# The first mixer of a one-core block: decay matrices applied one slot later, by 64 weight columns to their own half of the partitions

## What is computed

```python
def step(state, inp):                                   # chunks of 128 positions
    xc, dtc, lac, bc, cc = inp
    cum = jnp.cumsum(lac, axis=1)
    decay = jnp.exp(jnp.where(causal, cum[:, :, None] - cum[:, None], -jnp.inf))
    xdt = xc * dtc[..., None]
    cb = jnp.einsum('blgn,bsgn->blsg', cc, bc)
    y = jnp.einsum('blsgr,bsgrp->blgrp', cb[..., None] * decay, xdt)
    y = y + jnp.einsum('blgn,bgrpn->blgrp', cc, state) * jnp.exp(cum)[..., None]
    ...
```

## Time and profile before

| | us |
|---|---|
| median of 3 runs | 1860.97 (1857.37 to 1861.91) |
| profiled execution, device time | 1857.3 |
| its span | 1855.6 |
| TensorE matmul busy | 1735.0 (94%) |
| VectorE busy | 1189.9 (64%) |
| ScalarE busy | 769.0 (41%) |
| GpSimd busy | 408.1 (22%) |
| mean granted clock of TensorE | 0.983 |

### The profile page before, as it was taken

How to read it: one execution, slowest core, us unless ns; L and a number is a source line. 1 busy time by engine, 2 the same in 40 slices (tenths; PEclk the granted TensorE clock), 3 DMA queues, 4 the chain that set the end, 5 groups by cost and what they waited for, 6 DMA issues and landing times.

```text
span 1855.6 us, 21247 instructions
## 1 busy us (share of the span) xinstructions
PE 1735.0 (94%) x8104; PEld 1404.2 (76%) x8104; DVE 1189.9 (64%) x1587; ACT 769.0 (41%) x1143; POOL 408.1 (22%) x351
## 2 busy tenths in 40 slices
PE   6989999999987999999999889999999999999997
PEld 4767777787765777878777677888778778888886
DVE  6868878877966747575757676777665553434343
ACT  5333444343343435444445344446454442324232
POOL 0444644653563100000002501222120110000001
PEclk9989999999988999999999899999999999999999
DMA  3312222222210322222212223222323233333331
GB/s 102 91 35 68 67 70 57 60 66 69 57 49 25 86 54 65 80 79 69 76 54 87 63 74 80 62 59 80 103 82 103 88 91 91 103 91 102 92 101 69
DMA packets 253772, 139.18 MB, mean 75 GB/s; under 512 B 26013, under 2 KB 248134, under 8 KB 253670
## 3 DMA queue, kind: packets, MB, share of 16 engines
q1 hardware_dynamic: 253670, 137.82, 26.1%
HBM read 135.70 MB, written 2.10 MB: 74 GB/s over the span
## 4 chain that ended last, share of the span: by engine, by line
PE 58%; DVE 22%; ACT 9%; issue 7%; POOL 4%; DMA 1%; ACTq 0%; DVEq 0%; SPq 0%; POOLq 0%
PE stream L79 16%; PE stream L81 16%; PE stream L80 16%; DVE weights_lo L147 3%; ACT weights_hi L137 2%; DVE ssd_x L983 2%; DVE ssd_work L1061 1%; DVE ssd_bc L983 1%; DVE ssd_work L1057 1%; DVE ssd_y L1088 1%; PE q L1978 1%; PE q L2002 1%; POOL ssd_y L653 1%; PE q L79 1%; PE q L81 1%
## 5 line engine op out<-in xcount | busy, mean ns | idle before, releaser
L79 PE MATMUL stream<-u_lo,weights_hi 128*128 128x512 f32 (+2 forms) x1312 | 525.3, 400 | 17.0 <-DVE h L952 5.1
L81 PE MATMUL stream<-u_hi,weights_hi 128*128 128x512 f32 (+2 forms) x1312 | 514.7, 392 | 0.0
L80 PE MATMUL stream<-u_hi,weights_lo 128*128 128x512 f32 (+2 forms) x1312 | 514.6, 392 | 0.0
L147 DVE TENSOR_TENSOR weights_lo<-weights_raw,weights_hi 128x1024 fp32r<-128x1024 f32 (+4 forms) x269 | 336.3, 1252 | 270.2 <-ACT weights_hi L137 269.9
L137 ACT ACTIVATE weights_hi<-weights_raw 128x1024 fp32r<-128x1024 f32 (+4 forms) x269 | 268.5, 1000 | 444.9 <-PE stream L81 430.4
L79 PEld LDWEIGHTS stream<-u_lo,weights_hi 128*128 128x128 f32 (+2 forms) x1312 | 247.7, 189 | 81.0 <-issue 12.4
L81 PEld LDWEIGHTS stream<-u_hi,weights_hi 128*128 128x128 f32 (+2 forms) x1312 | 247.3, 188 | 54.2 <-issue 0.4
L80 PEld LDWEIGHTS stream<-u_hi,weights_lo 128*128 128x128 f32 (+2 forms) x1312 | 247.4, 189 | 53.9 <-issue 2.9
L217 POOL COPY h_sum_of_squares<-h_squares 128x512 f32<-128x512 f32 x5 | 3.2, 648 | 796.9 <-ACT h_squares L205 796.9
L79 PE MATMUL stream<-mlp_a_lo,weights_hi 128*128 128x512 f32 x256 | 100.2, 391 | 0.0
L81 PE MATMUL stream<-mlp_a_hi,weights_hi 128*128 128x512 f32 x256 | 99.7, 389 | 0.0
(11 more groups left out here) (484 smaller groups left out, 3155.9 us busy)
## 6 DMA issues: line engine op xcount, KB each, us to landing
weights_raw<-in_w_mlp_dram SPq DMA_DIRECT2D x64, 512.0 KB, 4.0
weights_raw<-in_ssd_w_in_dram SPq DMA_DIRECT2D x48, 512.0 KB, 3.9
weights_raw<-in_gla_w_in_dram SPq DMA_DIRECT2D x40, 512.0 KB, 3.8
weights_raw<-in_w_in_dram SPq DMA_DIRECT2D x29, 512.0 KB, 3.8
weights_raw<-in_ssd_w_out_dram SPq DMA_DIRECT2D x16, 512.0 KB, 3.6
weights_raw<-in_gla_w_out_dram SPq DMA_DIRECT2D x13, 512.0 KB, 3.4
weights_raw<-in_w_out_dram SPq DMA_DIRECT2D x8, 512.0 KB, 3.9
weights_raw<-in_w_xkv_dram SPq DMA_DIRECT2D x8, 512.0 KB, 3.8
```

The lines of the kernel that those rows point to most:

```text
L79: pe.matmul(out, lh, rl, start=first, stop=False, skip_group_check=skip)
L80: pe.matmul(out, ll, rh, start=False, stop=False, skip_group_check=skip)
L81: return pe.matmul(out, lh, rh, start=False, stop=last, skip_group_check=skip)
L147: dve.tensor_tensor(lo, raw_view(c, n), hi.bitcast(F32), ALU.subtract).then_inc(c.w_split, 1)
```

## The change

In `y_intra`, `y_intra(g, t)` is called in slot t + 3 instead of t + 2: slots 3 to 6. Each product now has the head's own 64 columns as stationary operand and writes 64 partitions of the bank, 0 to 63 for the first head of a pair and 64 to 127 for the second; none adds to another. `x_pair` loses its zeros (128 columns a pair), the copies into it become two instead of four, the semaphore counts on them follow, and GpSimd's clear and its semaphore go.

```diff
-        xp = mb("x_pair", [P, NT, 2, 192])
+        xp = mb("x_pair", [P, NT, 2, P])
...
-            pool.memset(xp[:, :, :, 64:128], 0.0).then_inc(s_clear, 1)
...
             def y_intra(g, t):
                 pe.wait_ge(s_m, 3 * (4 * g + t + 1))
                 if t == 0:
-                    pe.wait_ge(s_xp, 5 * g + 5)
+                    pe.wait_ge(s_xp, 3 * g + 3)
                     pe.wait_ge(s_xw, 4 * g + 4)
                 for p in range(2):
                     for h in range(2):
-                        a = slice(64 * h, 64 * h + P)
-                        last = pe.matmul(q[p][:, t * P:(t + 1) * P], xp[:, t, p, a], mm[:, t % 2, 2 * p + h, :],
-                                         start=h == 0, stop=h == 1, skip_group_check=True)
+                        a = slice(HD * h, HD * (h + 1))
+                        last = pe.matmul(q[p][a, t * P:(t + 1) * P], xp[:, t, p, a], mm[:, t % 2, 2 * p + h, :],
+                                         start=True, stop=True, skip_group_check=True)
                 last.then_inc(s_y, 1)
...
-                if 2 <= k <= 5:
-                    y_intra(g, k - 2)
+                if 3 <= k <= 6:
+                    y_intra(g, k - 3)
...
-                    act.wait_ge(s_clear, 1)
                     if g:
                         act.wait_ge(s_y, 4 * g)
                     for b in range(2):
-                        for h in range(2):
-                            src = q[b][:, :].rearrange("p (t j h m) -> p t j h m", t=2, j=2, h=2)[:, :, :, h, :]
-                            act.activation(xp[:, 2 * b:2 * b + 2, :, P * h:P * h + 64], src, ACT.Copy)\
-                               .then_inc(s_xp, 1)
+                        src = q[b][:, :].rearrange("p (t j m) -> p t j m", t=2, j=2)
+                        act.activation(xp[:, 2 * b:2 * b + 2, :, :], src, ACT.Copy).then_inc(s_xp, 1)
...
-                    dve.wait_ge(s_xp, 5 * g + 4)
+                    dve.wait_ge(s_xp, 3 * g + 2)
```

More of the change, by code:

```diff
@@ L596, in ssd_stage @@
          s_arg, s_decay, s_t2, s_m, s_y, s_con, s_st, s_int, s_e, s_ee, s_asm, s_sq, s_nrm,
-         s_rs, s_yn, s_yh, s_yl, s_clear) = (sem(n) for n in (
+         s_rs, s_yn, s_yh, s_yl) = (sem(n) for n in (
              "centre_tap", "taps", "conv_done", "gate_done", "transposed", "cb_products",
@@ L601, in ssd_stage @@
              "states", "y_inter", "cum_spread", "exp_cum_ready", "assembled",
-             "squared", "square_sums", "rstd_ready", "normed", "y_rounded", "y_rest", "cleared"))
+             "squared", "square_sums", "rstd_ready", "normed", "y_rounded", "y_rest"))
         G = range(SG)
```

## The result

| | before | after |
|---|---|---|
| median | 1861.44 (1857.37 to 1863.25, 4 runs) | 1848.21 (1846.92 to 1849.49, 4 runs) |
| profiled execution | 1857.3 | 1846.9 |
| one steady round of the first mixer | 65.74 | 64.39 |

The account below looks back on a forecast made before the run. The prediction took VectorE's stretch from 281 to 300 us of the first mixer's round as the bound; first round 5.8, six rounds 7.8 and last 0.5 made 14.1 us off 1860.97: 1846.9, given as 1846.5, range 1839 to 1856.

Parts of the forecast that it names:

- VectorE is the bound, TensorE's stalls are its shadow: Steady round: VectorE's stretch from 281 to 300 us sets the time; TensorE's 22.8 us of block waits are no gain yet.
- 1.3 us a steady round: Slots 2 to 4: earlier GpSimd steps collide less with VectorE, 1.3 us a round, 7.8 us over six rounds.
- just fits: Fourth block in slot 6 costs 0.81 us; two later TensorE waits for VectorE give back 0.4 each.
- First round 5.8, or 4.4 if the idleness lowers the clock again: First round: decay sums start 4.4 us earlier; 1.4 more if the clock stays at 2.4 GHz, making 5.8.
- Last round 0.5: Last round: L724 no longer stands behind the block of t=3, 0.5 us; otherwise the move gives nothing there.
- The block stays 0.81: TensorE's block: 64-column products into their own halves leave its 0.81 us unchanged, change 0.
- Halves side by side, 1843.7: Rival, chance 0.27: a block's halves overlap on TensorE, block 0.41 us, 3.2 us more gain, 1843.7.
- The waits only move: Rival, chance 0.15: GpSimd's earlier start hits other VectorE work, the 1.3 vanishes, first and last round remain: 1854.7.
- Slower, by a switch of 0.9 us or more: Rival, chance 0.05: switching to half-wide tiles in TensorE's blocks costs 0.9 us extra or more; at 1.2, 1866.

Follow-up runs that it names:

- e12: Kernel before the change, nothing moved or narrowed, with the last of GpSimd's four step tensors written by ScalarE; 1848.9 us, steady round 64.20.
- e3: Changed kernel with GpSimd's four steps of slot 4 held until VectorE's second tap of the tile in front; 1860.4 us, steady round 65.45.
- e1: Kernel before with only the block moved one slot later, products still 128 wide with the zeros; 1849.4 us, steady round 64.48.
- e4: Changed kernel with each block's loops reordered, both products of the lower half first, then both of the upper; 1849.2 us, rounds of 64.4.
- e13: Changed kernel with two GpSimd step tensors and the first state copy on ScalarE, and blocks back at full width with zeros; 1828.0 us, against 1827.2 narrow.
- e5: Changed kernel with VectorE's first state copy done by ScalarE in slot 3; 1850.0 us, steady round 64.40.
- e9: Changed kernel with one of GpSimd's four step tensors and VectorE's first state copy on ScalarE; 1840.7 us, steady round 64.13.
- e7: Changed kernel with the four products of each block done twice; rounds 1.57 us longer.
- e8: Changed kernel with the last of GpSimd's four step tensors written by ScalarE; 1842.0 us, steady round 64.12.

## Why the prediction was right, and where not

Forecast 1846.5, measured 1848.2, within the range; 14.1 us worked out, 13.2 measured.

- *VectorE is the bound, TensorE's stalls are its shadow.* Right. The waits at the block fell from 22.8 to 1.8, and those of the stream for banks grew from 5.5 to 16.2 ("from 5 to about 15" was forecast). e12 left the stalls and took the gain; e3 left the order and lost it.
- *1.3 us a steady round.* Right, 64.4 as forecast, in its parts as well: L147 of slot 4 at 1.45 (1.45 forecast), the mask's addition at 0.69 (0.69), 0.8 won at L147 of slot 3 (0.83) and 0.7 lost at L1091 (0.63). Six rounds gave 7.7 against 7.8. That the block moved into slot 6 "just fits" held as well: the waits of L794 for L1033 that were to give it back fell from 3.0 us to 0.6.
- *First round 5.8, or 4.4 if the idleness lowers the clock again.* The step that failed is the choice between the two. TensorE waited 3.09 us ahead of the sums at 96.53, and from 97.4 to 100.8 the granted clock was 0.50, the 1.2 GHz level; the sums to the block at the end of slot 5 took 8.2 us, where they took 7.85 before, not 6.48. The gain was 4.5, the other end. The sums themselves came at 96.53, where 97.3 was forecast: GpSimd's first step for them began at 92.00 instead of 92.8, and 0.4 of this is the shorter opening. That made up for the 8.2, so that 4.5 lies so close to 4.4 is partly luck.
- *Last round 0.5.* It showed 94.2 against 93.8 in the profiled pair, with 30.7 us of low clock in it against 23.9. e1, with 23.9 us of low clock in it as before, took 93.2, 0.6 less. One execution each: the 0.5 is likely, not shown.
- *The block stays 0.81.* The sum was nearly right for a wrong reason. I had argued from a step of width in the lower half that narrowness neither gains nor costs. It does both. TensorEngine Tiling in the Trainium skill has both in it, the gain (Theoretical Speedup) and the drain on a change of mode (Key Properties); the records show a body of 0.385 instead of 0.779 and 0.27 us more at the two edges, which fits a drain but doesn't prove it. They nearly cancel for a block of four. On the clock of the kernel: 1.1 us between e1 and after (1849.4, 1848.2), inside their spread.
- *Halves side by side, 1843.7.* Products of a block do overlap, but that the two halves are what runs side by side is not shown (e4), and the price was wrong: it left out the edges, and took TensorE for the bound of the round eight times, while e13 shows 0.05 a block even where TensorE is nearly full.
- *The waits only move.* Wrong here, but its mechanism, VectorE or GpSimd arriving at another meeting and the gain lost there, is what e5 and e9 show of other edits. (The 0.7 that the rival's text counts as lost in slot 3 lies in slot 2, at L1091.)
- *Slower, by a switch of 0.9 us or more.* The edges are 0.27 us.

## What to carry to other kernels

When the same instruction has two lengths in a timeline, look at the other engine of the shared port before counting its work: here 1.3 us of a 66 us round lay in four such meetings, and moving GpSimd's start in slot 4 by 1.4 us against VectorE's taps (from 1.71 us behind their start to 0.34), or giving one of its operations to ScalarE in the kernel before, was worth 1.3 to 1.5 us a round, while the changed order of TensorE without the move of GpSimd (e3) gave 0.3. Work saved on VectorE pays only if it doesn't bring VectorE sooner into such a meeting; e5 gained nothing, and the same edit 3.8 us once GpSimd was out of the way. A long wait in the list of waits is a place to begin, not a gain: of 21.0 us that went at the block, 10.7 came back at the next thing TensorE asked of VectorE and 7.2 at GpSimd's steps.

## What the hardware showed that was not expected

- Narrow products into halves of the partitions: starts in pairs 7 ns apart, half the body time, with 0.09 us more ahead and 0.17 us more behind a block. A block of four products gains 0.13 us by it. For eight, e7's records give 1.33 us from the last start ahead to the first behind, against an estimate of 1.92 at full width (1.026 and eight records more at 0.112).
- A VectorE operation with two SBUF inputs of 0.69 us takes 1.41 and one of 1.22 takes up to 2.05 beside GpSimd, and GpSimd's goes from 1.04 to 2.02, while the taps (3.09 to 3.11) and the additions to h (0.67 to 0.68), which read PSUM, keep their lengths.
- In the first round a TensorE wait of 3.1 us was followed by 3.4 us at the 1.2 GHz level, a wait of 4.75 by 6.8. In e8 a wait of 2.17 at the same place had no such stretch behind it. The length doesn't follow the wait alone: e3's wait of 4.79 had 3.4 us at the low level behind it.
